# A chunked RWKV scan in f32: VectorE transposes the running inverse, and both directions share the four quarters of TensorE's array

## What is computed

```
def step(s, inp):
    r_t, w_t, k_t, v_t, a_t, b_t = inp          # a = -kk, b = kk * a
    sa = jnp.einsum('bhvk,bhk->bhv', s, a_t)
    s = s * w_t[:, :, None, :] + sa[..., None] * b_t[:, :, None, :] + v_t[..., None] * k_t[:, :, None, :]
    return s, jnp.einsum('bhvk,bhk->bhv', s, r_t)
```

## Time and profile before

| | |
|---|---|
| median of three runs | 2737.98 us |
| the profiled execution | 2736.92 us |
| its span in the trace | 2735.1 us |
| the 16 pairs | about 102 us to 1132 us of the span |
| one pair in the middle | 64.56 us |

### The profile page before, as it was taken

How to read it: one execution, slowest core, us unless ns; L and a number is a source line. 1 busy time by engine, 2 the same in 40 slices (tenths; PEclk the granted TensorE clock), 3 DMA queues, 4 the chain that set the end, 5 groups by cost and what they waited for, 6 DMA issues and landing times.

```text
span 2735.1 us, 67041 instructions
## 1 busy us (share of the span) xinstructions
PE 2643.8 (97%) x29878; PEld 1866.5 (68%) x29878; DVE 1039.0 (38%) x2286; ACT 713.9 (26%) x1515; POOL 412.1 (15%) x439
## 2 busy tenths in 40 slices
PE   5999999999999999899999999999999999999998
PEld 1677777777777777666888674445544458785787
DVE  4644544444444554334364132112711113331512
ACT  3333333333333433113221121002410013101401
POOL 2433333333333332000001000000000001000000
PEclk9999999999999999999999999999999999999999
DMA  6211111111111111463444742221043343441252
GB/s 241 78 36 36 36 36 43 36 36 43 37 42 36 36 36 50 156 224 89 142 132 146 273 150 77 69 63 57 32 132 122 116 158 116 131 139 58 83 154 92
DMA packets 82070, 257.61 MB, mean 94 GB/s; under 512 B 11607, under 2 KB 19384, under 8 KB 81080
## 3 DMA queue, kind: packets, MB, share of 16 engines
q1 hardware_dynamic: 75176, 241.89, 27.4%
q10 hardware_dynamic: 6000, 8.28, 0.8%
q0 software_dynamic: 608, 3.15, 0.3%
HBM read 252.23 MB, written 1.05 MB: 93 GB/s over the span
## 4 chain that ended last, share of the span: by engine, by line
PE 56%; DVE 1%; ACT 1%; DMA 0%; issue 0%; DVEq 0%; ACTq 0%
PE ps L1844 13%; PE ps L2013 9%; PE ps L1788 8%; PE ps L1724 6%; PE ps L2030 5%; PE ps L1878 4%; PE ps L1669 1%; PE ps L1918 1%; PE ps L1958 1%; PE ps L1938 1%; PE ps L1903 1%; PE ps L1745 1%; PE ps L1733 1%; PE ps L1898 1%; PE ps L1765 1%; PE ps L1821 1%
## 5 line engine op out<-in xcount | busy, mean ns | idle before, releaser
L1844 PE MATMUL ps<-h,ring 128*128 128x256 f32 (+1 forms) x1184 | 363.5, 465 | 0.0
L1844 PEld LDWEIGHTS ps<-h,ring 128*128 128x128 f32 x1184 | 225.0, 190 | 126.2 <-issue 107.1
L2013 PE MATMUL ps<-h,ring 128*128 128x512 f32 (+1 forms) x768 | 256.1, 486 | 0.0
L1788 PE MATMUL ps<-h,ring 128*128 128x256 f32 x1024 | 225.2, 379 | 0.8 <-ACT general L2176 0.8
L1788 PEld LDWEIGHTS ps<-h,ring 128*128 128x128 f32 x1024 | 193.9, 190 | 34.5 <-issue 7.7
L2013 PEld LDWEIGHTS ps<-h,ring 128*128 128x128 f32 x768 | 145.2, 190 | 103.0 <-issue 93.2
L561 PE MATMUL ps<-ring,general 128*128 128x128 f32 x1024 | 150.8, 284 | 0.5 <-DVE general L1237 0.3
L993 ACT ACTIVATE general<-ps 128x256 f32<-128x256 f32 (+1 forms) x192 | 82.0, 427 | 247.7 <-PE ps L702 246.9
L1175 DVE TENSOR_TENSOR general<-general,ps 128x128 f32<-128x128 f32 x320 | 74.7, 282 | 161.6 <-PE ps L728 161.5
L542 PE MATMUL ps<-general,ring 128*128 128x512 f32 x256 | 133.1, 606 | 0.8 <-issue 0.8
L2030 PE MATMUL ps<-general,ring 128*128 128x512 f32 (+1 forms) x384 | 131.0, 486 | 0.0
(11 more groups left out here) (353 smaller groups left out, 4179.1 us busy)
## 6 DMA issues: line engine op xcount, KB each, us to landing
ring<-in_w_mods SPq DMA_DIRECT2D x96, 512.0 KB, 5.1
ring<-in_w_feature SPq DMA_DIRECT2D x74, 512.0 KB, 3.5
ring<-in_w_rkvg SPq DMA_DIRECT2D x64, 512.0 KB, 3.8
ring<-in_w_in SPq DMA_DIRECT2D x48, 512.0 KB, 3.5
ring<-in_w_merge SPq DMA_DIRECT2D x48, 512.0 KB, 3.5
ring<-in_w_out SPq DMA_DIRECT2D x32, 512.0 KB, 5.6
ring<-in_w_token SPq DMA_DIRECT2D x24, 512.0 KB, 3.9
ring<-in_w_merge SPq DMA_DIRECT2D x48, 256.0 KB, 3.1
```

Source lines behind the costliest of these rows:

```text
L1788: mm = pe.matmul(ps[:, n % 4, 0:NX], weights(key, k), R.h[:, k, 0:NX], start=(k == 0), stop=(k == KD - 1))
L1844: mm = pe.matmul(ps[:, j % 4, 0:width], weights(("feature", l, j), k), R.h[:, k, cols], start=(k == 0), stop=(k == KD - 1))
L2013: mm = pe.matmul(ps[:, 2 * b, 0:NQ], weights(key, k), R.h[:, k, 0:NQ], start=(k == 0), stop=(k == KD - 1))
```

## The change

- `turn_inverse` moves from TensorE and ScalarE to VectorE: `dve.transpose` turns 32x32 blocks of `T` into `U`, one instruction for z = 0 and two (one per half of the partitions, into the other half) for z = 1, at the start of each level. Up to level 4 no block of the inverse is larger than 32.
- Level 5 no longer grows `T`: a 32x32 product of `Y` and `U` gives the missing block of the transposed inverse, and VectorE adds it straight into `U`. The turn for the sixth time is gone.
- `below`, `grow`, `seen_values` and `solve` are one loop over both directions, with z innermost. The half that is written (`below`) or read (`grow`) is now `solved_in(z, p)`, and the bank follows h, no longer the half that is read.
- `X0` is computed at level 5, in banks 6 and 7, and ScalarE copies it out. The solve writes `AT`'s part and `X0`'s part to banks of their own.
- The keys and reads are turned in banks 6 and 7; the reads use all four quarters (64 matmul records in one batch). `first_blocks` splits its 128-column products into two of 64.
- Fills are let through by a number of columns (`fill(part, FILL_...)`).
- VectorE's `scan(m, 0)`, `scan(m, 1)` and `difference(m)` stand at levels 1, 2 and 4 instead of 1, 1 and 2; `floor(m)` behind level 5.

```
+    def turn_inverse(i, l):
+        for z in range(2):
+            if l == 1:
+                dve.wait_ge(Z("eye_out")[z], i + 1)
+            else:
+                dve.wait_ge(Z("t_out")[z], (LAST - 1) * i + l - 1)
+            if z == 0:
+                last = dve.transpose(W.U[:, 0], W.T[:, 0])
+            else:
+                for p in range(2):
+                    a, g = oth(p), solved_in(1, p)
+                    last = dve.transpose(W.U[g:g + 64, 1], W.T[a:a + 64, 1])
+            last.then_inc(Z("u_out")[z], 1)
...
+def solved_in(z, p):
+    return nat(p) if z else oth(p)
...
         for cc in range(4):
             a = oth(cc % 2)
-            for h in range(2):
-                mm = pe.matmul(ps[:, bank + h, 64 * cc:64 * cc + 64], W.bk[rows(h), z, 4 + cc, :],
-                               W.ar[rows(h), z, 4 + cc, a:a + 64], start=True, stop=True)
+            for g in range(2):
+                for h in range(2):
+                    mm = pe.matmul(ps[rows(g), bank + h, 64 * cc:64 * cc + 64], W.bk[rows(h), z, 4 + cc, rows(g)],
+                                   W.ar[rows(h), z, 4 + cc, a:a + 64], start=True, stop=True)
...
+    def grow(i, l):
...
+                        if l < LAST:
+                            mm = pe.matmul(ps[a:a + 64, b0 + h, j * P:j * P + 32], W.U[g:g + 64, z, q, :], W.Y[g:g + 64, z, q, :],
+                                           start=True, stop=True)
+                        else:
+                            t, c = 32 - 32 * z, 32 * z
+                            own = slice(g + t, g + t + 32)
+                            mm = pe.matmul(ps[g + c:g + c + 32, b0 + h, j * P:j * P + 32], W.Y[own, z, q, :], W.U[own, z, q, t:t + 32],
+                                           start=True, stop=True)
...
         for l in range(1, LAST + 1):
-            if l == 1 and ahead:
-                scan(m, 0)
+            turn_inverse(i, l)
             for z in range(2):
                 mask_level(i, z, l)
             if l == 1:
                 if i:
                     variance(i - 1)
                 if ahead:
-                    scan(m, 1)
+                    scan(m, 0)
             if l == 2 and ahead:
-                difference(m)
+                scan(m, 1)
             if l == 3:
                 if i:
                     affine(i - 1)
                 bonus_weights(i)
-            if l == 5 and ahead:
-                floor(m)
+            if l == 4 and ahead:
+                difference(m)
             for z in range(2):
                 add_level(i, z, l)
```

More of the change, by code:

```diff
@@ L416 @@
 LAST = 5
+FILL_MASKS = 1000
+FILL_BELOW = (0, 1000, 1000, 1000, 1100, 500)
+FILL_GROWN = (0, 1100, 800, 1000, 800, 800)
+FILL_SOLVED = 800
+FILL_MOVES = 500
+FILL_STATES = 512
 PAIR_SEMS = (
@@ L630, in between @@
         keys = key_pieces(m) if ahead else iter(())
+        key = lambda: 512 if next(keys, None if not ahead else 1) is None else 0
         for z in range(2):
@@ L633, in between, with fill @@
                 turn_keys(i, z, half)
-                yield
-                next(keys, None)
-                yield
-        for z in range(2):
-            turn_reads(i, z)
-            yield
-            next(keys, None)
-            yield
+                yield 290
+            yield key()
+        turn_reads(i)
+        yield 640
+        for _ in range(4):
+            yield key()
         if i:
-            pe.wait_ge(at_out[1], i + 1)
+            second_bank(i)
             turn_out(i - 1)
-            yield
+            yield 290
         for _ in keys:
-            yield
+            yield 512
         bonus_weights(i)
-        yield
+        yield 250
         if not ahead:
             return
+        if not i:
+            second_bank(i)
         for n, _ in enumerate(value_pieces(m)):
+            yield 290
             if n == 6:
                 norm(m)
-                yield
-            yield
+                yield 512
         for _ in read_pieces(m):
-            yield
+            yield 256
+    def fill(part, columns):
+        for done in part:
+            columns -= done
+            if columns <= 0:
+                return
     def first_blocks(i, z):
@@ L697, in strict, with below @@
         return W.Ac[r0:r0 + 64, z, h, ch - 4, :]
[L699 removed]
+    def below(l):
         for j in range(4):
[L701 to L718 removed]
@@ new lines, in seen_values @@
+    def seen_values(i):
+        for z in range(2):
+            pe.wait_ge(v_in[z], i + 1)
+            pe.wait_ge(at_out[z], i + 1)
+        pe.wait_ge(s["coef_out"], i + 1)
+        for j in range(4):
+            for h in range(2):
+                for p in range(2):
+                    r, ch = nat(p), chunk_of(j, p)
+                    for z in range(2):
+                        g, n = solved_in(z, p), (4 * h + j) * 64
+                        mm = pe.matmul(ps[g:g + 64, 6 + z, n:n + 64], strict(z, h, ch, r), W.VZ[r:r + 64, z, ch, rows(h)],
+                                       start=True, stop=True)
+                        if (j, h, p) == (3, 1, 1):
+                            mm.then_inc(Z("x0_done")[z], 1)
@@ new lines, in solve @@
+    def solve(i):
+        for z in range(2):
+            pe.wait_ge(u_out[z], 6 * (i + 1))
+        for n, right, done in ((0, W.AT, Z("wa_done")), (1, W.X0, Z("wu_done"))):
+            if n:
+                for z in range(2):
+                    pe.wait_ge(x0_out[z], i + 1)
+            for j in range(4):
+                for h in range(2):
+                    for p in range(2):
+                        a = oth(p)
+                        for z in range(2):
+                            g, q = solved_in(z, p), 4 * h + j
+                            mm = pe.matmul(ps[a:a + 64, 2 + 2 * z + n, q * 64:q * 64 + 64], W.U[g:g + 64, z, q, :], right[g:g + 64, z, q, :],
+                                           start=True, stop=True)
+                            if (j, h, p) == (3, 1, 1):
+                                mm.then_inc(done[z], 1)
@@ L887, in pairs_pe @@
             own_reads(i, z)
-        next(part, None)
+        fill(part, FILL_MOVES)
         for n in range(1, NCH):
@@ L895, in pairs_pe @@
             if n < NCH - 1:
-                next(part, None)
-                next(part, None)
+                fill(part, FILL_STATES)
         mm.then_inc(s["ysum_done"], 1)
@@ L908, in pairs_act @@
     ps = R.ps
[L909 removed]
+    low_done, t2_out, bk_done = Z("low_done"), Z("t2_out"), Z("bk_done")
     chunks = lambda ap: ap.rearrange("p (c t) -> p c t", t=C)
@@ L1285, in pairs_dve @@
                 bonus_weights(i)
-            if l == 5 and ahead:
-                floor(m)
+            if l == 4 and ahead:
+                difference(m)
             for z in range(2):
                 add_level(i, z, l)
-            if l == 5 and ahead:
-                pack_keys(m, 0)
-        for z in range(2):
-            seen(i, z)
+        if ahead:
+            floor(m)
+            pack_keys(m, 0)
         if ahead:
```

249 lines of the change are left out of this document (92 added, 157 removed), and 2 rows, old and new, of the table PAIR_SEMS.

## The result

The changed kernel takes 2742.67 us (median of 20 runs, 2738.68 to 2753.95) against 2737.70 us (20 runs, 2733.38 to 2742.32) of the kernel before: a ratio of 1.0022, 95% interval 1.0014 to 1.0030. That is 5 us slower where 73 us faster was forecast, and outside the range. The profiled execution has a span of 2741.9 us.

A forecast was written before the change was run, and what follows sets the result against it. TensorE's own queue was taken as the bound in all but the last pair. Gains of 59.5 us in pairs 1 to 14, 5.0 in pair 0 and 8 in the last, total 72.5, gave 2665 us, range 2608 to 2712.

The forecast's parts named there:

- What bounds the kernel: Middle pairs, 64.56 us each: TensorE's queue sets the time, so removed instructions shorten the pair unless a new wait appears.
- What the change removes: TensorE, per pair: turns of the inverse 5.2, first blocks 1.0, reads 1.05, last level's product 0.4; sum 7.65 us.
- Level 5's product: TensorE at the last level: the new 32x32 product takes 0.69 us against 1.07, saving 0.4 us per pair.
- Transposes: VectorE, three per level, 15 per pair: ordinary price assumed, 0.60 + 0.60 + 0.68 = 1.88 us per level.
- Rival 2: VectorE's transposes are dear: gain gone at 1.1 us a turn, about 2793 us at the scan's 1.45; chance 0.08.
- The chain between levels: VectorE's 3.9 us between growing products fits under TensorE's work at each level, with 0.4 to 1.4 us to spare.
- The wait at the norm: Norm matmul after level 4 waits for GpSimd's squares, delayed by the moved difference: 3.4 us per pair, pair 0 2.7.
- The last pair: The dependent chain through VectorE and ScalarE sets its time: 45 us against 55.25, of which 8 us gain was taken.
- The sum: Whole kernel: pairs 1 to 14 gain 4.25 us each, pair 0 5.0, last pair 8; total 72.5 us.
- Rival 1: The wait ahead of the norm matmul is covered, so all 15 waits fall away: 2615 us; chance 0.12.
- Rival 3: Row halves of TensorE's array writing one PSUM bank can't overlap, in 12 groups per pair: about 2841 us; chance 0.03.
- Rival 5: TensorE's removed work does not show because another engine takes its place entirely: 2738 us; chance 0.03.

The follow-up runs named there:

- Experiments 6 to 8: Changed kernel, GpSimd's squares first: large matmuls spread between small runs, 2667.27 us; or first blocks whole, 2668.62 us. Kernel before with only first blocks split: 2735.18 us.
- experiment 1: Changed kernel with GpSimd's squares of the scaled keys moved ahead of the decay sum and the gating: 2685.65 us, ratio 0.9803.
- Experiment 11: Changed kernel with GpSimd's squares first, and direction 0's VectorE transpose split into two instructions of 64 partitions: 2720.50 us, ratio 0.9934.

## Where the prediction went wrong, point by point

**What bounds the kernel.** "An instruction taken from it shortens the pair by its issue-to-issue time, as long as nothing new has to be waited for" is the sentence that failed. It held for time taken by large matmuls. It did not hold for an edit that makes small ones denser: TensorE then stood idle with nothing to wait for in the program. Experiments 6 to 8 show that the density and order of the records make these gaps; that the supply of code is what runs short rests on the match of times and on the return every three pairs. Nor did it hold for the clock, which fell behind the new wait. As to the gaps, the trace of before already showed issue gaps (0.2 to 2.6 us, mostly in the last pair), and I read them only as a doubt on the last pair. In the sum I wrote that they "may come back", and gave that some 2 us there (8 taken of 10) and nothing in the 14 pairs before it, where they came to 33.0 us.

**What the change removes.** From the middle pair before (64.56) to the shortest of experiment 1 (57.67) it is 6.9 us instead of 7.65. Start-to-start sums by line over these two pairs show that what was priced is there: turns of the inverse 5.5 (forecast 5.2), first blocks 1.2 to 1.3 (1.0; some of its records are missing from the trace), reads 1.07 (1.05). Level 5's product takes 0.68 us for its 64 records in 7 of the changed kernel's pairs, as forecast, and 0.78 to 0.94 in the other 8 ahead of the last, so it gives 0.1 to 0.4. What was missing is on the other side, in lines that the forecast left as they were: the reads of the states (L849) took 0.7 us more, 0.2 of it a small new wait, the solve 0.4 more, half of it a gap, the next pair's keys 0.2 more; reads and gates took 0.3 less. Why, apart from the wait and the gap, no run shows.

**Transposes.** 0.70 us against 0.68: right. The Trainium skill's figure for a bf16 transpose (VectorE: DVE Perf Modes, "The three transpose paths", 311 ns for 128x128) is for another type and size, bf16 and 128 columns against f32 and 512 elements a lane here, so this trace does not test it. Rival 2 fell with it.

**The chain between levels.** It fits with the transposes as they are: in the changed kernel 2.0 us of waits ahead of all growing products and 1.9 ahead of the strict ones. Experiment 11 says that it fits more narrowly than the forecast's 0.4 us of slack.

**The wait at the norm.** The place, the releaser and the length were right: 3.61 us in the middle pairs, forecast 3.4. In pair 0 it was 4.47, forecast 2.7: there the fills run ahead, for no previous output is turned, and the norm stands ahead of level 4's growing product (135.01 and 137.43 us) and not behind it. What was missing is what a wait does to the engine behind it: with the clock at 1.2 GHz for the next records a pair loses 0.9 us more net, and the last pair, where TensorE waits often, has a granted clock of 0.73 where the earlier trace rows had 0.94. The forecast treated TensorE's speed as given.

**The last pair.** Forecast 8 us less, measured 1.6 more. Its busy time is less by 2 us only, and 6.3 us of gaps are left of 7.6. At a granted clock of 0.73 TensorE runs at 1.2 GHz for over half of it, against an eighth before (0.94). How much of the 9.6 us each of these is, and whether the chain through VectorE was sized rightly, no run here settles; the last pair took 55.8 to 58.3 us in every version of the changed kernel.

**The sum.** Pairs 1 to 14 were to gain 59.5 us and lost 11.3, so 70.8 are missing. A pair without gaps takes 62.14 instead of the forecast 60.3 (64.56 - 4.25): 14 x 1.83 = 25.6, made of 0.2 for the wait, 0.9 for the clock behind it and 0.75 for the lines that cost more than before. All 14 together take 50.0 us more than 14 times the shortest: 33 are gaps (2 before), the other 17 mostly slower records at the lower clock; in the pair from 425.08 on the gaps sum to 5.5 us and the excess to 8.9, with a granted clock of 0.90. Less the 4.8 us by which the pairs before exceeded 64.56, that is 25.6 + 50.0 - 4.8 = 70.8. The last pair misses 9.6, pair 0 misses 2.3, and behind the loop both kernels are the same to 3.5 us.

**The rivals.** Rival 1 could not be, the wait was there; experiment 1 shows what it would have given: 2686, not 2615, with 57.9 us of gaps in it. Rival 3 (quarters of one bank) did not come true: 64 records of L734 or L749, whose row halves now share banks, take 1.07 us as before; the rule of the Trainium skill (TensorEngine Tiling (Array Packing), "Gotcha 1: PSUM Pressure") is not borne out for these shapes. (In that rival's text, 64 of 512 columns of a record of 0.48 us are 0.06 us and not 0.053; the argument stands.) Rival 5 named the right size for a wrong reason: the place of the removed work was taken, but by no engine. No rival of mine was "TensorE itself is slower".

## What to carry over

Where an engine is busy for the whole span, ask what its rate rests on before you count busy time as gain: here, by all that the runs show, the supply of its own code, and a clock that fell when it stood still. If the "issue" row of the waits is not empty before a change, price an edit that swaps few large matmuls for many small ones with it, and place the small ones so that a large one stands between two runs. A wait on the busiest engine costs its length and the slower records behind it; look for the producer whose order on its own queue makes it, here one line on GpSimd worth 57 us.

## What the hardware showed that I had not expected

- What I take for TensorE's code comes as packets of some 16 KB, each taking about 1 us (2.1 at most). In runs of small matmuls at 16.7 ns a record TensorE then stood for 0.3 to 3.7 us, five times at about the 107th record of the solve, each time three pairs on. With weight transfers of 512 KB beside it the longest were 3.0 us, with small ones 1.7.
- The version without the wait at the norm has more gaps, 57.9 us against 39.3 with it.
- The same idle time of 2.1 us left the clock at 2.4 GHz in one pair and at 1.2 GHz in another. Single pairs can't be priced by it, only their share: all 15 of the changed kernel at 3.5 us and more, 10 of 14 at 2.93, 5 of 14 at 1.9 to 2.1, 2 of 14 at 0.65 to 0.75.
- A VectorE transposition of 64 partitions takes as long as one of 128 (L1189 707 and L1185 704 ns at 512 f32 elements a lane).
